# Linear attention scan of a two-layer hybrid block: six query scalings in one VectorE instruction, the decay column copied by ScalarE

## The chip, the cores and the metric

One NeuronCore of one Trainium2 chip runs the whole program. The metric is the device time of one execution in microseconds (us). Each execution is one launch; a version is judged by the median of its timed runs. One execution is also recorded by the hardware profiler, and all rows below come from that one record.

## The reference

The block has two layers. Each normalises 1024 latent and 256 context tokens, projects them, runs four mixers (differential attention, mLSTM, gated linear attention, windowed attention), gates and projects back. The change touches the gated linear attention (GLA) alone:

```
def _gla_step(smat, xs):          # one chunk of one direction, all heads
    q, k, v, la = xs
    bc = jnp.cumsum(la, axis=2)
    inter = jnp.einsum('bhtd,bhdv->bhtv', q * jnp.exp(bc), smat)
    rel = jnp.where(tril[:, :, None], bc[:, :, :, None, :] - bc[:, :, None, :, :], -jnp.inf)
    a = jnp.einsum('bhtd,bhtsd,bhsd->bhts', q, jnp.exp(rel), k)
    o = inter + jnp.einsum('bhts,bhsv->bhtv', a, v)
    b_end = bc[:, :, -1]
    smat = jnp.exp(b_end)[..., None] * smat + jnp.einsum('bhsd,bhsv->bhdv', k * jnp.exp(b_end[:, :, None] - bc), v)
    return smat, o
```

It runs forward and backward over context and latents, with 4 heads of 32 key and 64 value channels. The decay is different for each channel and token, so that q and k have to be scaled by exponentials before they are multiplied.

## The kernel before, in words

Tokens are cut into 10 tiles of 128, and each tile is visited once in each direction: 20 units a layer, in the order of the list UNITS, which alternates the two directions. The arrays q and k lie transposed (128 channels by tokens, qT and kT). For unit u the scan does five things.

- TensorE, `exponents(u)` (lines 1219 to 1224): six matmuls sum the log decays into eight 128x128 maps in PSUM banks 4 and 5.
- ScalarE (L1206): one Exp over all eight maps (128x1024) into `decays`, which has two places (u % 2) in the tile yT.
- GpSimd: `kx` = decays 1 to 5 times kT (L1194, 128x640), and place 0 from decay 0 and the token-major k (L1196, 128x128). VectorE, `scale_q(u)`: the last column of decay 7 is copied to `start` (L1303, 128x1, four places); `qx` = decays 2 to 6 times qT (L1304, 128x640, two places); `from_start` = decay 7 times qT (L1306, 128x128, three places).
- TensorE, `levels(u)` (L1237, L1242, L1248): the score maps of four heads at several distances, from kx and qx into PSUM banks 0 to 3. `fresh(u)` (L1260): the new state's sum from kx place 0. `out(u)`: from_start times the state (L1271), plus the picked scores times v (L1274).
- VectorE: three masked copies of the scores from PSUM into `acc`, here called the picks (L1335, 128x512 each). Then `finish(u)`: the state is scaled by `start` and the new sum added (L1312), and the output is copied to or added to yT (L1318 or L1316). After a wait for its own writes it marks `finished`.

The order on each engine is written out by hand. TensorE: exponents(0), exponents(1), then for each u levels(u), fresh(u), exponents(u+2), out(u-1), and last out(19). VectorE, for each u: finish(u-2), scale_q(u+1), picks(u). GpSimd and ScalarE take the units in turn. Semaphores tie them: levels(u) waits for its kx and qx and for the picks of u-1 (whose PSUM banks it overwrites); picks(u) wait for levels(u); finish(u) waits for out(u) and fresh(u); Exp(u) waits for the exponents and for both scalings of u-2; scale_q(u) waits for Exp(u), for levels(u-2) and, from u = 3, for out(u-3).

No DMA that the scan waits for is issued in it, and a barrier of all engines closes it. One scan runs in each layer; the two are at 409 to 522 us and 1774 to 1887 us of the record.

Of the kernel before, what the change touches and what calls it, by code (L numbers as in the profile page):

```python
# [999 lines left out]
def stage_gla(nc, env):  # L1000
# [3 lines left out]
    with outer:  # L1004
# [19 lines left out]
        with ExitStack() as own, nc.Block() as block:  # L1024
# [101 lines left out]
            def _(dve):  # L1126
# [21 lines left out]
                for n, b in enumerate(BLOCKS):  # L1148
# [3 lines left out]
                dve.wait_ge(k_kept.sem, 3)  # L1152


        (sums_ready, expo_mm, decay_ready, k_scaled, q_scaled, map_mm, picked, o_mm, u_mm, finished, zeroed, cleared, dv2) = (
            signal(n) for n in ("c_sums_ready", "c_expo_mm", "c_decay", "c_k_scaled", "c_q_scaled", "c_map_mm",
                                "c_picked", "c_out_mm", "c_new_mm", "c_finished", "c_zeroed", "c_cleared", "c_dve2"))
        NU = len(UNITS)
        with ExitStack() as own, nc.Block() as block:
            def tile(name, shape, dt=F32):  # L1160
                return own.enter_context(env["sbuf"](name, shape, dt))

            sums = tile("c_sums", [P, 2, 8 * P], F32R)
            decays = yT[:, 6:8, :].rearrange("p a t -> p (a t)")[:, 0:2 * 8 * P].rearrange("p (u n t) -> p u n t", u=2, n=8)
            kx = tile("c_kx", [P, 2, 6, P])
            qx = tile("c_qx", [P, 2, 5, P])
            from_start = tile("c_from_start", [P, 3, P])

            spare = env["ring"][:, S_AV % RING, KT * SLAB_W[S_AV]:]
            acc = spare[:, 0:2 * HEADS * P].rearrange("p (w h t) -> p w h t", w=2, h=HEADS)  # L1170
            state = spare[:, 2 * HEADS * P:2 * HEADS * P + 2 * GW].rearrange("p (w c) -> p w c", w=2)
            start = tile("c_start", [P, 4])

            def out_bank(u):
                return ps[:, 6 + u % 2, 0:GW]
# [4 lines left out]
            def span(u):  # L1180
                return slice(UNITS[u][2] * P, (UNITS[u][2] + 1) * P)

            @block.gpsimd
            def _(pool):
                pool.tensor_copy(sums[:, 1, :], sums_in[:, 8 * P:]).then_inc(sums_ready.sem, 1)
                pool.wait_ge(sums_ready.sem, 2)
                pool.memset(acc[:, :, :, :], 0.0).then_inc(zeroed.sem, 1)
                pool.memset(state[:, :, :], 0.0).then_inc(zeroed.sem, 1)
                for u in range(NU):
                    pool.wait_ge(decay_ready.sem, u + 1)  # L1190
                    if u >= 2:
                        pool.wait_ge(map_mm.sem, u - 1)
                        pool.wait_ge(u_mm.sem, u - 1)
                    pool.tensor_tensor(kx[:, u % 2, 1:6, :], decays[:, u % 2, 1:6, :],  # L1194
                                       kT[:, span(u)].unsqueeze(1).broadcast_to([P, 5, P]), ALU.mult).then_inc(k_scaled.sem, 1)
                    pool.tensor_tensor(kx[:, u % 2, 0, :], decays[:, u % 2, 0, :], k_tok[:, UNITS[u][2], :], ALU.mult)\  # L1196
                        .then_inc(k_scaled.sem, 1)

            @block.scalar
            def _(act):  # L1200
                for u in range(NU):
                    act.wait_ge(expo_mm.sem, u + 1)
                    if u >= 2:
                        act.wait_ge(k_scaled.sem, 2 * (u - 1))
                        act.wait_ge(q_scaled.sem, 2 * (u - 1))
                    act.activation(decays[:, u % 2, :, :], ps[:, 4:6, :].rearrange("p b (n t) -> p (b n) t", n=4), ACT.Exp)\  # L1206
                       .then_inc(decay_ready.sem, 1)

            @block.tensor
            def _(pe):  # L1210
# [15 lines left out]

                def levels(u):
                    way, i, j = UNITS[u]
                    q, k = qx[:, u % 2, :, :], kx[:, u % 2, :, :]
                    pe.wait_ge(k_scaled.sem, 2 * u + 1)  # L1230
                    pe.wait_ge(q_scaled.sem, 2 * u + 1)
                    if u >= 1:
                        pe.wait_ge(picked.sem, 3 * u)
                    for n, (a, b) in enumerate(((4, 2), (5, 3), (1, 4))):
                        for h in range(HEADS):
                            r = slice(32 * h, 32 * h + 32)
                            pe.matmul(ps[:, h, n * P:(n + 1) * P], k[r, a, :], q[r, b, :], start=True, stop=True,  # L1237
                                      tile_position=(32 * h, 0))
                    s0, t0 = (0, 64) if way == 0 else (64, 0)
                    for h in range(HEADS):  # L1240
                        r = slice(32 * h, 32 * h + 32)
                        pe.matmul(ps[s0:s0 + 64, h, t0:t0 + 64], k[r, 2, s0:s0 + 64], q[r, 0, t0:t0 + 64],  # L1242
                                  start=True, stop=True, tile_position=(32 * h, s0))
                    for blk in (0, 64):
                        s0, t0 = (blk, blk + 32) if way == 0 else (blk + 32, blk)
                        for h in range(HEADS):
                            r = slice(32 * h, 32 * h + 32)
                            last = pe.matmul(ps[s0:s0 + 32, h, t0:t0 + 32], k[r, 3, s0:s0 + 32], q[r, 1, t0:t0 + 32],  # L1248
                                             start=True, stop=True, tile_position=(32 * h, s0))
                    last.then_inc(map_mm.sem, 1)  # L1250
# [13 lines left out]
                def out(u):  # L1264
# [2 lines left out]
                        pe.wait_ge(zeroed.sem, 2)  # L1267
                    if u >= 2:
                        pe.wait_ge(finished.sem, u - 1)
                    pe.wait_ge(q_scaled.sem, 2 * (u + 1))  # L1270
                    pe.matmul(out_bank(u), from_start[:, u % 3, :], state[:, way, :], start=True, stop=False, skip_group_check=True)  # L1271
                    pe.wait_ge(picked.sem, 3 * (u + 1))
                    for h in range(HEADS):
                        last = pe.matmul(out_bank(u)[:, h * DH:(h + 1) * DH], acc[:, way, h, :], vC[:, j, h * DH:(h + 1) * DH],  # L1274
# [15 lines left out]
            def _(dve):  # L1290
# [3 lines left out]
                def scale_q(u):  # L1294
                    way, i, j = UNITS[u]
                    dve.wait_ge(decay_ready.sem, u + 1)
                    if u >= 2:
                        dve.wait_ge(map_mm.sem, u - 1)
                    if u >= 3:
                        dve.wait_ge(o_mm.sem, u - 2)  # L1300
                    end = P - 1 if way == 0 else 0
                    d = decays[:, u % 2, :, :]
                    dve.tensor_copy(start[:, u % 4:u % 4 + 1], d[:, 7, end:end + 1])  # L1303
                    dve.tensor_tensor(qx[:, u % 2, :, :], d[:, 2:7, :], qT[:, span(u)].unsqueeze(1).broadcast_to([P, 5, P]), ALU.mult)\  # L1304
                       .then_inc(q_scaled.sem, 1)
                    dve.tensor_tensor(from_start[:, u % 3, :], d[:, 7, :], qT[:, span(u)], ALU.mult).then_inc(q_scaled.sem, 1)  # L1306

                def finish(u):
                    way, i, j = UNITS[u]
                    dve.wait_ge(u_mm.sem, u + 1)  # L1310
                    dve.wait_ge(o_mm.sem, u + 1)
                    dv2.mark(dve.scalar_tensor_tensor(out=state[:, way, :], in0=state[:, way, :], scalar=start[:, u % 4:u % 4 + 1],  # L1312
# [1137 lines left out]
```

## Time and profile before

| | |
|---|---|
| three timed runs | 2673.01, 2687.75, 2691.18 us; median 2687.75 |
| the profiled execution's own time | 2683.7 us |
| its span | 2681.9 us (1.8 us lie around it) |
| mean granted TensorE clock | 0.88 of full speed |
| TensorE matmul busy | 2151.8 us, 80% of the span |
| VectorE busy | 1867.3 us, 70% |
| ScalarE busy | 1129.8 us, 42% |
| GpSimd busy | 411.4 us, 15% |

An engine's busy share is an average over eight stages a layer with different limits, so it does not say what bounds the scan. The granted clock is 1.00 where TensorE runs at 2.4 GHz and 0.50 where it runs at 1.2 GHz. In the rows, PE is TensorE's matmuls, PEld its weight loads, DVE is VectorE, ACT is ScalarE, POOL is GpSimd; L1304 is line 1304.

### The profile page before, as it was taken

The page shows a single profiled execution, that of the slowest core. Times are in us where ns is not written, and L with a number is a line of the kernel's source. Part 1 is how long each engine was busy: PE and PEld are TensorE (multiplying, and loading weights), DVE is VectorE, ACT ScalarE, POOL GpSimd, SP SyncE. Part 2 cuts the span into 40 slices and gives each one's busy share as a digit, 9 for nine tenths or more (in the row PEclk, how much of TensorE's full clock was granted, in tenths as well). Part 3 has the DMA queues.
Part 4 walks back from the last instruction along what each step waited for, and adds up shares of the span by engine and source line. Part 5 has one row for each costly group of instructions (what it writes and reads, how often), then busy time and mean ns, then how long its engine had stood idle before and what let it go on. Part 6 is the DMA issues. An engine that isn't in the chain of part 4 may idle for free. (4 is left out here: it accounts for less than half of the span.)

```text
span 2681.9 us, 38569 instructions
## 1 busy us (share of the span) xinstructions
PE 2151.8 (80%) x14712; PEld 1804.3 (67%) x14712; DVE 1867.3 (70%) x3533; ACT 1129.8 (42%) x2196; POOL 411.4 (15%) x410
## 2 busy tenths in 40 slices
PE   4968798786888785899978778879767977858988
PEld 2857676666677664787857567767655866647877
DVE  2585667778878567755745766669698786667757
ACT  4433351333667534633224443432435666346321
POOL 0002204322000011022110004025031000110222
PEclk7978896898898797999988889969788989979999
DMA  8100010000000100001433000100000001000021
GB/s 322 74 16 1 17 48 2 2 1 1 1 1 1 48 32 1 29 36 39 153 138 120 16 16 2 48 16 2 1 0 1 1 1 48 16 17 27 37 104 54
DMA packets 18182, 99.80 MB, mean 37 GB/s; under 512 B 2128, under 2 KB 2256, under 8 KB 12752
## 3 DMA queue, kind: packets, MB, share of 16 engines
q1 hardware_dynamic: 12816, 87.89, 8.6%
q10 hardware_dynamic: 5184, 9.44, 0.9%
q8 instruction: 119, 1.95, 0.3%
q14 instruction: 63, 0.52, 0.1%
HBM read 87.88 MB, written 9.44 MB: 36 GB/s over the span
## 5 line engine op out<-in xcount | busy, mean ns | idle before, releaser
L1807 DVE TENSOR_REDUCE a_st<-ps 128x1 f32<-128x1280 f32 (+1 forms) x144 | 196.9, 1370 | 23.2 <-PE ps L1719 22.7
L1778 ACT ACTIVATE ring<-ps,a_st 128x1280 f32<-128x1280 f32 (+1 forms) x144 | 177.3, 1232 | 74.6 <-DVE a_st L1807 74.4
L454 PE MATMUL ps<-a_proj_wh,a_proj_xh 128*128 128x512 f32 (+1 forms) x320 | 119.2, 373 | 62.5 <-DVE a_proj_xl L435 61.6
L2090 PE MATMUL ps<-g_x_hi,g_w_hi 128*128 128x512 f32 (+1 forms) x400 | 148.4, 371 | 10.0 <-DVE g_x_lo L2151 9.5
L2091 PE MATMUL ps<-g_x_lo,g_w_hi 128*128 128x512 f32 (+1 forms) x400 | 147.7, 369 | 0.0
L2092 PE MATMUL ps<-g_x_hi,g_w_lo 128*128 128x512 f32 (+1 forms) x400 | 147.6, 369 | 0.0
L1719 PE MATMUL ps<-a_k,a_q 128*128 128x512 f32 (+1 forms) x400 | 123.8, 419 | 26.1 <-ACT ring L1778 21.6
L2151 DVE TENSOR_TENSOR g_x_lo<-hT,g_x_hi 128x512 fp32r<-128x512 f32 (+1 forms) x120 | 84.5, 709 | 85.3 <-ACT g_x_hi L2114 83.8
L2114 ACT ACTIVATE g_x_hi<-hT 128x512 fp32r<-128x512 f32 (+1 forms) x120 | 70.3, 589 | 158.3 <-PE ps L2092 151.2
L1734 PE MATMUL ps<-cst,ring 128*128 128x128 f32 x656 | 107.8, 299 | 27.0 <-ACT a_aT L1787 15.1
L418 ACT ACTIVATE b_proj_xh<-hT 128x640 fp32r<-128x640 f32 (+1 forms) x64 | 63.8, 1003 | 147.4 <-PE ps L454 145.0
L2225 PE MATMUL ps<-o_w_hi,o_y_hi 128*128 128x512 f32 x288 | 114.1, 396 | 13.5 <-DVE o_y_lo L2256 7.2
L2164 POOL TENSOR_TENSOR yT<-yT,g_gate 128x512 f32<-128x512 f32 (+1 forms) x50 | 61.3, 1232 | 382.5 <-DVE g_gate L2129 236.7
L454 PEld LDWEIGHTS ps<-a_proj_wh,a_proj_xh 128*128 128x128 f32 x320 | 68.7, 215 | 75.3 <-issue 48.9
L454 PE MATMUL ps<-a_proj_wl,a_proj_xh 128*128 128x512 f32 (+1 forms) x320 | 116.2, 363 | 0.0
L454 PE MATMUL ps<-a_proj_wh,a_proj_xl 128*128 128x512 f32 (+1 forms) x320 | 115.8, 362 | 0.0
L2226 PE MATMUL ps<-o_w_lo,o_y_hi 128*128 128x512 f32 x288 | 113.5, 394 | 0.0
L2227 PE MATMUL ps<-o_w_hi,o_y_lo 128*128 128x512 f32 x288 | 113.3, 393 | 0.0
L1734 PEld LDWEIGHTS ps<-cst,ring 128*128 128x128 f32 x656 | 81.4, 153 | 46.5 <-ACT a_aT L1787 22.9
L454 PE MATMUL ps<-b_proj_xh,b_proj_wh 128*128 128x512 f32 (+1 forms) x192 | 76.9, 401 | 44.4 <-DVE b_proj_xl L435 38.0
L418 ACT ACTIVATE a_proj_xh<-hT 128x640 fp32r<-128x640 f32 x64 | 46.6, 741 | 147.9 <-PE ps L454 145.6
L2282 ACT ACTIVATE o_y_hi<-yT 128x640 fp32r<-128x640 f32 (+1 forms) x64 | 43.5, 686 | 152.5 <-PE ps L2227 144.6
(363 smaller groups left out, 6397.9 us busy)
## 6 DMA issues: line engine op xcount, KB each, us to landing
ring<-in_w SPq DMA_DIRECT2D x22, 2048.0 KB, 7.5
yT<-in_w SPq DMA_DIRECT2D x4, 2048.0 KB, 9.8
latents<-hT ACTq DMA_DIRECT2D x32, 256.0 KB, 2.0
ring<-in_w SPq DMA_DIRECT2D x6, 1024.0 KB, 5.0
hT<-in_tok SPq DMA_DIRECT2D x10, 512.0 KB, 15.5
hT<-in_tok SPq DMA_DIRECT2D x20, 256.0 KB, 5.9
hT<-latents SPq DMA_DIRECT2D x16, 256.0 KB, 6.5
cst<-in_cst SPq DMA_DIRECT2D x1, 2688.0 KB, 14.6
```

The lines of the kernel that those rows point to most:

```text
L418: act.activation(self.x_hi[:, i % self.BUFS, 0:m], self.env["hT"][:, k, t0:t0 + m], ACT.Copy).then_inc(self.hi.sem, 1)
L454: last = pe.matmul(out, left, right, start=k == 0 and j == 0, stop=k == KT - 1 and j == 2)
L1719: last = pe.matmul(ps[:, 3 * c + b, 0:w], q4[:, 2 * h + c, t * P:(t + 1) * P], k4[:, 2 * h + c, k0:k0 + w], start=True, stop=True)
L1734: last = pe.transpose(ps[:, 6 + n % 2, (k - a) * P:(k - a + 1) * P], p(u, 0, T)[:, k * P:(k + 1) * P], C(env, "ident"))
L1778: act.activation(p(u, c, n), ps[:, 3 * c:3 * c + 3, :].rearrange("p b n -> p (b n)")[:, 0:n], ACT.Exp, bias=st[:, 0:1], accum_out=st[:, 1: ...
L1807: dve.tensor_reduce(stat[:, u % SLOTS, c, 0:1], ps[:, 3 * c:3 * c + 3, :].rearrange("p b n -> p (b n)")[:, 0:n], AX.X, ALU.max, negate=Tru ...
L2090: pe.matmul(out, w_hi[:, k, cols], x_hi[:, at, 0:b[1]], start=k == 0, stop=False)
L2091: pe.matmul(out, w_hi[:, k, cols], x_lo[:, at, 0:b[1]], start=False, stop=False)
L2092: last = pe.matmul(out, w_lo[:, k, cols], x_hi[:, at, 0:b[1]], start=False, stop=k == KT - 1)
L2225: pe.matmul(ps[:, n % 8, :], y_hi[:, at, tile], w_hi[:, at, :], start=k == 0, stop=False)
L2226: pe.matmul(ps[:, n % 8, :], y_hi[:, at, tile], w_lo[:, at, :], start=False, stop=False)
L2227: last = pe.matmul(ps[:, n % 8, :], y_lo[:, at, tile], w_hi[:, at, :], start=False, stop=k == KT - 1)
```

## The change

`decays` leaves yT: place 0 becomes a tile of its own and place 1 goes to the spare part of the ring, where `state` was; `state` becomes a tile of its own. `qx` moves into yT, has three places instead of two and six maps instead of five, and takes the place of `from_start`. VectorE makes all six products in one instruction (128x768). The copy of the decay column moves from VectorE to ScalarE, as an activation (Copy) behind the Exp, with a semaphore `start_kept` for which `finish` waits. The counts of `q_scaled` go by one a unit instead of two; scale_q(u) waits for levels(u-3) instead of levels(u-2).

```diff
-            decays = yT[:, 6:8, :].rearrange("p a t -> p (a t)")[:, 0:2 * 8 * P].rearrange("p (u n t) -> p u n t", u=2, n=8)
             kx = tile("c_kx", [P, 2, 6, P])
-            qx = tile("c_qx", [P, 2, 5, P])
-            from_start = tile("c_from_start", [P, 3, P])
+            qx = yT[:, 6:8, :].rearrange("p a t -> p (a t)")[:, 0:3 * 6 * P].rearrange("p (u n t) -> p u n t", u=3, n=6)
...
-            state = spare[:, 2 * HEADS * P:2 * HEADS * P + 2 * GW].rearrange("p (w c) -> p w c", w=2)
+            decays = [tile("c_decays", [P, 8, P]), spare[:, 2 * HEADS * P:2 * HEADS * P + 8 * P].rearrange("p (n t) -> p n t", n=8)]
+            state = tile("c_state", [P, 2, GW])
...
             def _(act):
...
                     if u >= 2:
                         act.wait_ge(k_scaled.sem, 2 * (u - 1))
-                        act.wait_ge(q_scaled.sem, 2 * (u - 1))
-                    act.activation(decays[:, u % 2, :, :], ps[:, 4:6, :].rearrange("p b (n t) -> p (b n) t", n=4), ACT.Exp)\
+                        act.wait_ge(q_scaled.sem, u - 1)
+                    act.activation(decays[u % 2][:, :, :], ps[:, 4:6, :].rearrange("p b (n t) -> p (b n) t", n=4), ACT.Exp)\
                        .then_inc(decay_ready.sem, 1)
+                    end = P - 1 if UNITS[u][0] == 0 else 0
+                    act.wait_ge(decay_ready.sem, u + 1)
+                    if u >= 4:
+                        act.wait_ge(finished.sem, u - 3)
+                    act.activation(start[:, u % 4:u % 4 + 1], decays[u % 2][:, 7, end:end + 1], ACT.Copy).then_inc(start_kept.sem, 1)
...
                 def levels(u):
-                    q, k = qx[:, u % 2, :, :], kx[:, u % 2, :, :]
+                    q, k = qx[:, u % 3, :, :], kx[:, u % 2, :, :]
                     pe.wait_ge(k_scaled.sem, 2 * u + 1)
-                    pe.wait_ge(q_scaled.sem, 2 * u + 1)
+                    pe.wait_ge(q_scaled.sem, u + 1)
...
-                    pe.wait_ge(q_scaled.sem, 2 * (u + 1))
-                    pe.matmul(out_bank(u), from_start[:, u % 3, :], state[:, way, :], start=True, stop=False, skip_group_check=True)
+                    pe.wait_ge(q_scaled.sem, u + 1)
+                    pe.matmul(out_bank(u), qx[:, u % 3, 5, :], state[:, way, :], start=True, stop=False, skip_group_check=True)
...
                 def scale_q(u):
                     dve.wait_ge(decay_ready.sem, u + 1)
-                    if u >= 2:
-                        dve.wait_ge(map_mm.sem, u - 1)
                     if u >= 3:
+                        dve.wait_ge(map_mm.sem, u - 2)
                         dve.wait_ge(o_mm.sem, u - 2)
-                    end = P - 1 if way == 0 else 0
-                    d = decays[:, u % 2, :, :]
-                    dve.tensor_copy(start[:, u % 4:u % 4 + 1], d[:, 7, end:end + 1])
-                    dve.tensor_tensor(qx[:, u % 2, :, :], d[:, 2:7, :], qT[:, span(u)].unsqueeze(1).broadcast_to([P, 5, P]), ALU.mult)\
+                    dve.tensor_tensor(qx[:, u % 3, :, :], decays[u % 2][:, 2:8, :], qT[:, span(u)].unsqueeze(1).broadcast_to([P, 6, P]), ALU.mult)\
                        .then_inc(q_scaled.sem, 1)
-                    dve.tensor_tensor(from_start[:, u % 3, :], d[:, 7, :], qT[:, span(u)], ALU.mult).then_inc(q_scaled.sem, 1)
 
                 def finish(u):
+                    dve.wait_ge(start_kept.sem, u + 1)
                     dve.wait_ge(u_mm.sem, u + 1)
                     dve.wait_ge(o_mm.sem, u + 1)
```

## Rows read from the trace of the kernel before

**Rows 1.** Busy time by stretch (us, PE, PEld, DVE, ACT, POOL, clock, DMA), first scan.
```profile
430.00:440.00 10.00, 10.00 (x130) 8.36 (x129) 6.22 (x14) 1.02 (x1) 2.64 (x4) 0.50 0.01 2
...
450.00:460.00 10.00, 9.29 (x186) 7.84 (x179) 9.13 (x18) 2.05 (x2) 5.80 (x6) 1.00 0.02 4
```

**Rows 2.** Waits in 449 to 510 us: who waited, total us, times, longest.
```profile
ACT yT L1206 <- PE ps L1224: 45.9, 13, 3.6
...
PE ps L1237 <- DVE ring L1335: 5.0, 14, 0.4
```

**Rows 3.** Timeline, one full-clock iteration: start us, us, engine, line, idle before.
```profile
449.03 0.46 DVE L1312 SCALAR_TENSOR_TENSOR ring<-ring,c_start,ps 128x256 f32<-128x256 f32 x1
...
502.55 1.00 PE L1274 MATMUL ps<-yT,ring 128*128 128x64 f32 x8
...
503.42 1.55 POOL L1194 TENSOR_TENSOR c_kx<-yT,c_kT 128x640 f32<-128x640 f32 x1 [2.01 <-ACT yT L1206]
503.66 0.48 DVE L1312 SCALAR_TENSOR_TENSOR ring<-ring,c_start,ps 128x256 f32<-128x256 f32 x1
...
503.87 0.95 PE L1237 MATMUL ps<-c_qx,c_kx 32*128 32x128 f32 x24 [0.32 <-DVE ring L1335]
504.06 0.42 DVE L1316 TENSOR_TENSOR yT<-ps,yT 128x256 f32<-128x256 f32 x1
504.72 0.15 DVE L1303 COPY c_start<-yT 128x1 f32<-128x1 f32 x1 [0.24 <-DVE yT L1316]
...
504.79 0.86 DVE L1304 TENSOR_TENSOR c_qx<-yT,c_qT 128x640 f32<-128x640 f32 x1
...
505.57 0.55 DVE L1306 TENSOR_TENSOR c_from_start<-yT,c_qT 128x128 f32<-128x128 f32 x1
...
506.04 2.25 DVE L1335 COPY_PREDICATED ring<-cst,ps 128x512 f32<-128x512 uint32 x3
...
507.07 1.00 PE L1274 MATMUL ps<-yT,ring 128*128 128x64 f32 x8
...
508.19 0.47 DVE L1312 SCALAR_TENSOR_TENSOR ring<-ring,c_start,ps 128x256 f32<-128x256 f32 x1
...
508.44 0.95 PE L1237 MATMUL ps<-c_qx,c_kx 32*128 32x128 f32 x24 [0.37 <-DVE ring L1335]
```

**Rows 4.** Durations ns, min/median/max, of single lines in 449 to 510 us.
```profile
L1304 DVE TENSOR_TENSOR c_qx<-yT,c_qT x14: 814/864/904, 450.1 to 509.3; 128x640 f32<-128x640 f32 x14
...
L1306 DVE TENSOR_TENSOR c_from_start<-yT,c_qT x13: 279/546/549, 450.9 to 505.6; 128x128 f32<-128x128 f32 x13
...
L1196 POOL TENSOR_TENSOR c_kx<-yT,c_k_tok x14: 460/1050/1069, 450.2 to 509.4; 128x128 f32<-128x128 f32 x14
```

**Rows 5.** Timeline, at the granted clock of 0.50 and where it rises.
```profile
437.48 0.48 DVE L1312 SCALAR_TENSOR_TENSOR ring<-ring,c_start,ps 128x256 f32<-128x256 f32 x1 [2.80 <-PE ps L1274]
...
442.90 1.81 PE L1274 MATMUL ps<-yT,ring 128*128 128x64 f32 x8
...
444.81 0.48 DVE L1312 SCALAR_TENSOR_TENSOR ring<-ring,c_start,ps 128x256 f32<-128x256 f32 x1 [2.79 <-PE ps L1274]
```

**Rows 6.** Timeline, the first units of the scan.
```profile
414.21 1.57 POOL L1194 TENSOR_TENSOR c_kx<-yT,c_kT 128x640 f32<-128x640 f32 x1 [2.01 <-ACT yT L1206]
414.23 2.22 DVE L1304 TENSOR_TENSOR c_qx<-yT,c_qT 128x640 f32<-128x640 f32 x1
...
419.75 0.55 DVE L1306 TENSOR_TENSOR c_from_start<-yT,c_qT 128x128 f32<-128x128 f32 x1
...
420.21 2.24 DVE L1335 COPY_PREDICATED ring<-cst,ps 128x512 f32<-128x512 uint32 x3
...
422.60 1.66 PE L1237 MATMUL ps<-c_qx,c_kx 32*128 32x128 f32 x24 [1.04 <-DVE ring L1335]
```

**Rows 7.** Timeline, levels of the last unit.
```profile
512.93 1.66 PE L1237 MATMUL ps<-c_qx,c_kx 32*128 32x128 f32 x24 [1.32 <-DVE ring L1335]
```

**Rows 8.** Line 995, a ScalarE Copy behind an Exp, whole record (ns min/median/max).
```profile
L995 ACT ACTIVATE yT<-ps,par x108: 360/424/523, 312.5 to 2277.2; 128x128 f32<-128x128 f32 x108
```

More of the change, by code:

```diff
@@ L1152, in _ @@
                 dve.wait_ge(k_kept.sem, 3)
-        (sums_ready, expo_mm, decay_ready, k_scaled, q_scaled, map_mm, picked, o_mm, u_mm, finished, zeroed, cleared, dv2) = (
+        (sums_ready, expo_mm, decay_ready, k_scaled, q_scaled, map_mm, picked, o_mm, u_mm, finished, zeroed, cleared, dv2, start_kept) = (
             signal(n) for n in ("c_sums_ready", "c_expo_mm", "c_decay", "c_k_scaled", "c_q_scaled", "c_map_mm",
-                                "c_picked", "c_out_mm", "c_new_mm", "c_finished", "c_zeroed", "c_cleared", "c_dve2"))
+                                "c_picked", "c_out_mm", "c_new_mm", "c_finished", "c_zeroed", "c_cleared", "c_dve2", "c_start_kept"))
         NU = len(UNITS)
@@ L1193, in _ @@
                         pool.wait_ge(u_mm.sem, u - 1)
-                    pool.tensor_tensor(kx[:, u % 2, 1:6, :], decays[:, u % 2, 1:6, :],
+                    pool.tensor_tensor(kx[:, u % 2, 1:6, :], decays[u % 2][:, 1:6, :],
                                        kT[:, span(u)].unsqueeze(1).broadcast_to([P, 5, P]), ALU.mult).then_inc(k_scaled.sem, 1)
-                    pool.tensor_tensor(kx[:, u % 2, 0, :], decays[:, u % 2, 0, :], k_tok[:, UNITS[u][2], :], ALU.mult)\
+                    pool.tensor_tensor(kx[:, u % 2, 0, :], decays[u % 2][:, 0, :], k_tok[:, UNITS[u][2], :], ALU.mult)\
                         .then_inc(k_scaled.sem, 1)
```

## The prediction

> **What bounds the kernel now.** The scan fills 112.9 us in each of the two layers, 226 of 2682 us, so I looked only there, first at the busy time by stretch. It shows two regimes [rows 1]. At a granted clock of 0.50 TensorE is busy without a gap. At 1.00 it is busy 93% and VectorE 91%: either could be the bound, and shares cannot say which. Next the waits [rows 2]: at full clock the levels' matmuls wait for the picks in each of 14 iterations, 0.36 us a time, while ScalarE has 3.5 us of idle time an iteration. Last the timeline of one iteration [rows 3], in which every start and end can be chained.
>
> The start of the finish's first instruction, L1312, moves from 449.03 to 508.19 in 13 iterations: 4.55 us each. Call E the end of the `out` matmuls, 502.55 + 1.00 = 503.55. VectorE's next steps, counted from E [rows 3]: L1312 at +0.11, the output at +0.51, the column copy at +1.17, qx at +1.24, from_start at +2.02, the picks at +2.49 to +4.74. The next but one `levels` starts at 508.44, +4.89, and TensorE needs 4.20 us from the start of levels to its own `out` end (503.87 to 507.07 + 1.00 = 508.07). This gives a **loop over two iterations**: out, finish, scalings, picks, levels, out. Its length is 4.89 + 4.20 = 9.09, or 4.545 an iteration. VectorE's own list, L1312 to L1312, takes 508.19 - 503.66 = 4.53. TensorE's own takes 4.20. So two loops bind at once, within 0.02 us. Shortening VectorE's list relieves the first as well, but the first holds the VectorE stretch only once in two iterations.
>
> **The change, part by part.**
>
> The column copy leaves VectorE: qx starts 0.07 after it [rows 3]. It saves at most 0.07 an iteration, and nothing where the port below decides.
>
> The two products become one. From the undisturbed lengths, 814 ns for 640 elements and 279 for 128 [rows 4], an element costs 535/512 = 1.045 ns. So 768 elements take 0.948, or 0.134 more than 640. from_start's slot goes: 506.04 - 505.57 = 0.47. It is so long because VectorE and GpSimd exclude each other here. L1306 takes 279 or 546 ns and L1196 460 or 1050 [rows 4], and in the first unit qx takes 2.22 where L1194 started 0.02 before it [rows 6]: it is through 0.67 after L1194's end. The slot thus was 0.20 of work and 0.27 of waiting for L1196.
>
> In the sum the same exclusion takes a part back. L1194 runs until 503.42 + 1.55 = 504.97, E + 1.42, because it follows Exp, which follows TensorE's exponents: it stands still against E. qx is ready at E + 1.17 now and has to wait until E + 1.42. It ended at 505.65, 0.68 after that, and will end 0.68 + 0.13 = 0.81 after, at E + 2.23; the picks start 0.08 before it is through (505.57 against 505.65), at E + 2.15 instead of 2.49. Gain 0.34 for each turn of the two-iteration loop: (9.09 - 0.34) / 2 = 4.375, **0.17 us an iteration**. VectorE's own list falls to about 4.53 - 0.34 = 4.19 and no longer binds alone. Without the exclusion the picks would start at E + 1.17 + 0.87 = E + 2.04, the gain would be 0.45 a turn. The Trainium skill, page "SBUF — State Buffer", says of the port pair that the two engines share that a VectorE instruction with two SBUF inputs and a GpSimd one exclude each other for their whole length. By that rule the first sum holds, without it the second; the trace agrees with the rule, by the 2.22 us above.
>
> Sum for one layer:
> - Start. The first picks wait for from_start of unit 1, 419.75, and begin at 420.21; merged they begin at about 419.75 + 0.13 = 419.88, 0.33 sooner. levels(1), 422.60, waits for them and for nothing else (1.04 idle) [rows 6]. Its qx waits for the same L1194 as now. -0.33. levels(0) waits for the wider qx, +0.13, but the picks behind it still begin later than it ends, so this is covered.
> - Clock of 0.50. An iteration is 7.33 long and VectorE waits 2.8 in it for `out` [rows 5]. The saving is hidden: 0.
> - Full clock, from the finish at 444.81 to that at 508.19, 14 iterations, 7 turns of the loop. Six save 0.34. The first is undisturbed by GpSimd (from_start took its shortest 0.28), so it saves 0.07 + 0.20 - 0.13 = 0.14. Together -2.18; I take -2.2.
> - Tail. levels(19) at 512.93 waits for picks(18) [rows 7], one more VectorE stretch behind the out end at 508.07. -0.34.
>
> That is -2.9 a layer, **-5.8 us** for both.
>
> At nothing I put: the ScalarE copy, 40 times. The nearest row is a Copy of 128x128 in 0.42 us behind an Exp, with no table load on its line [rows 8]; it lies in 3.5 us of idle time [rows 2], and a cost below nothing is excluded, since ScalarE does more. Its wait for finish(u-4) was met some 3 us before. If the cover were gone, each copy would delay the next Exp by at most 0.42 us. Behind Exp, GpSimd waits for decay_ready, which Exp itself still signals. The new wait of finish(u) for start_kept: the copy is done a full iteration before; the wait is issued while the last pick still runs. Between nothing and one semaphore step (0.11, out end to L1312) I take nothing; what queues behind it is all of VectorE's list, and at 0.11 a turn it would cost 7 x 0.11 a layer, 1.5 us in all. Three places of qx and the later levels wait (u-3 for u-2): VectorE never idled for it, 0. The widened qx holds L1196 up by 0.13, but fresh(u) needs it more than 3 us later. Moved tiles: no row prices an address; I take 0, and -1 to +1 us as ends. No DMA changes.
>
> **The rivals.**
>
> *A, the full width of VectorE's list.* If the end of `out` modelled in the trace is later than the real one, the two-iteration loop has slack and only the one-engine lists bind. VectorE's is then 4.53 - 0.47 - 0.07 + 0.13 = 4.12, TensorE's 4.20 + a step of 0.03, so TensorE paces at 4.23: 0.32 x 14 + 0.67 = 5.1 a layer, -10 us. For it: a matmul's end is modelled in the record, not seen. Against: out end to L1312 is 0.11 here and 444.81 - (442.90 + 1.81) = 0.10 where VectorE really waited [rows 5].
>
> *B, no gain.* TensorE at 93% is near its bound; if levels start later for another reason (kx, semaphores), the 0.17 vanishes: 0 to -2 us. Against: in all 14 iterations the wait ends with the picks [rows 2].
>
> *C, slower by the port.* qx wins the port now because it is already waiting when L1194 ends. If it comes after that, L1196 gets in first and qx waits another 0.46: picks at E + 1.42 + 0.46 + 0.81 - 0.08 = E + 2.61, against 2.49 now. The loop grows by 0.12 a turn, with the start's gain left: 7 x 0.12 - 0.33 = +0.5 a layer, **+1 us**, at worst +2. The point is qx ready later than E + 1.42; it is ready at E + 1.17, 0.07 sooner than now. The long L1306 is the rule (median 546), the short one the exception. Small.
>
> *D, the clock.* It rises when TensorE has run without a gap for some iterations [rows 1, 5]. The start's gap before levels(1) shrinks by 0.33 and everything after shifts. One iteration more at 0.50 costs 7.33 - 4.38 = 3 us a layer, and one fewer saves it: 2 x 3 on either side, -12 or 0. If later stages shift their rises too, slower by a few us is possible. The Trainium skill, "TensorE: Matmul & The Clock Gate", Part 1, says that idle TensorE is throttled and activity releases it; by that fewer gaps can only help, and I give the side of later rises less. This trace cannot tell them apart.
>
> **How the numbers follow.** The change is made against the profiled execution, 2683.7 us, which lies 4 us below the median of the three runs. The forecast for the profiled time is 2677.9, for the median 2687.75 - 5.8 = **2682 us**. The forecast itself, -4 to -7: 0.56. A: 0.12. B: 0.13. C: 0.05. D faster 0.07, D slower 0.07. The three runs spread over 18 us, more than any case; a median can move by that much with no change at all. The range goes from A on the lowest run (2673 - 10 = 2663, taken as 2665) to C on the highest (2691 + 2 = 2693). A change of less than 1% (27 us) can hardly be told from none in this kernel. Even all of 0.47 + 0.07 - 0.13 = 0.41 us in 40 units would be 16 us, so faster by over 1% needs the clock: 0.03. Slower by over 1% needs several later rises: 0.03. The rest, 0.94, is within 1%.
>
> **What would show it.** Right: L1312 to L1312 4.35 to 4.40 us at full clock; one qx row of 128x768 of 0.95 undisturbed and about 1.05 where it waits for L1194; picks at E + 2.15; the levels' wait for the picks down from 0.36 to about 0.18; a new wait of L1312 for `out` of 0.1 to 0.2; the same number of slow iterations; no second table load in the scan; each scan 110.0 instead of 112.9 us. Wrong: iterations of 4.23 (A), of 4.5 with TensorE's wait on something else (B), 0.46 us long L1196 before qx and picks at E + 2.6 (C), another count of 7.33 us iterations (D).

## The result and the profile after

| | us |
|---|---|
| before, median of 8 runs (2673.01 to 2691.18) | 2684.6 |
| changed, median of 8 runs (2650.28 to 2665.72) | 2658.6 |
| ratio of the runs | 0.9906, 95% interval 0.9883 to 0.9929 |
| forecast | 2682 (2665 to 2693), within 1% |

The time is below the range: some 25 us gained where 5.8 were forecast. A second timing gave 0.9925 (0.9907 to 0.9942), 20 us. The profiled run took 2660.28 us, 23.4 less than the one before. Two lines of its page:

```profile
span 2658.5 us, 38559 instructions
...
PE 2129.9 (80%) x14712; PEld 1785.4 (67%) x14712; DVE 1850.4 (70%) x3453; ACT 1137.3 (43%) x2236; POOL 418.2 (16%) x410
```

Where the time went is seen by cutting the span at the scans. Scan length here is from the first VectorE instruction to the start of the last finish (L1312). Each is a difference of two timeline rows; for the second scans these are 1886.47 - 1774.51 and 1864.27 - 1764.69.

| record | first scan | second scan | the rest of the span |
|---|---|---|---|
| before | 111.9 | 112.0 | 2458.0 |
| changed | 103.0 | 99.6 | 2455.9 |

So 21.3 of the 23.4 us lie in the scans of these two records. Inside them, first the steady part, which answers [rows 3]. This is the timeline of the changed kernel at full clock (start us, us, engine, line, idle before):

```profile
436.13 1.00 PE L1278 MATMUL ps<-yT,ring 128*128 128x64 f32 x8
...
437.00 1.55 POOL L1193 TENSOR_TENSOR c_kx<-ring,c_kT 128x640 f32<-128x640 f32 x1 [1.89 <-ACT ring L1205]
...
437.13 0.95 PE L1241 MATMUL ps<-yT,c_kx 32*128 32x128 f32 x24
437.27 0.48 DVE L1312 SCALAR_TENSOR_TENSOR c_state<-c_state,c_start,ps 128x256 f32<-128x256 f32 x1 [0.29 <-ACT c_start L1211]
...
438.33 1.05 DVE L1304 TENSOR_TENSOR yT<-ring,c_qT 128x768 f32<-128x768 f32 x1 [0.24 <-DVE yT L1316]
...
439.30 2.26 DVE L1335 COPY_PREDICATED ring<-cst,ps 128x512 f32<-128x512 uint32 x3
...
440.32 1.00 PE L1278 MATMUL ps<-yT,ring 128*128 128x64 f32 x8
...
441.45 0.48 DVE L1312 SCALAR_TENSOR_TENSOR c_state<-c_state,c_start,ps 128x256 f32<-128x256 f32 x1
```

With E = 436.13 + 1.00 = 437.13, L1312 stands at E + 0.14, qx at + 1.20, the picks at + 2.17 (forecast + 2.15). qx takes 1.05 because L1193 holds the port until 438.55. VectorE now waits 0.29 for `out`. The row names the column copy as releaser, since that ended last by the profile (437.16); but finish(u) needs the copy of its own unit, which was long done. Experiment 5 has no such copy, and there the same wait is put down to `out`. From 430 to 500 us of this record the levels wait for the picks 8 times in 16 iterations, 3.3 us in all or 0.21 an iteration (forecast 0.18), and L1312 waits in the others, 0.34 a time (forecast 0.1 to 0.2).

From levels(2) at 20.17 to levels(18) at 90.23 us of the first scan there are 16 iterations: 4.38 us each. Before, levels(4) to levels(18), 35.47 to 99.27, were 14 of 4.56. Forecast were 4.375 and 4.545.

Now the clock. Busy time by stretch (us, PE, PEld, DVE, ACT, POOL, clock, DMA), second scan of before, in the 17.0 us that follow 18.4 us after its begin:

```profile
1792.90:1809.90 17.00, 17.00 (x155) 14.65 (x153) 8.17 (x17) 3.07 (x3) 5.10 (x5) 0.50 0.00 1
1809.90:1873.70 63.80, 58.86 (x1010) 50.80 (x1009) 59.19 (x113) 14.34 (x14) 34.55 (x29) 1.00 0.01 2
```

The same stretch of the changed kernel, and the 4.8 us ahead of it:

```profile
1778.20:1783.00 4.80, 4.80 (x64) 3.94 (x61) 3.10 (x4) 0.34 (x2) 2.73 (x2) 0.50 0.02 3
1783.00:1800.00 17.00, 15.99 (x286) 13.88 (x285) 14.21 (x22) 4.72 (x8) 9.20 (x8) 1.00 0.01 2
```

In 17 us TensorE does 155 matmuls at 1.2 GHz and 286 at 2.4. Before, the rise comes 35.4 us after the begin of both scans; changed, 19.8 and 18.4 us after it. That is the larger part of the difference between these two records.

The head of the scan shows what the rise may hang on. Timeline of the changed kernel, its first units; they answer [rows 6]:

```profile
413.19 0.96 DVE L1304 TENSOR_TENSOR yT<-c_decays,c_qT 128x768 f32<-128x768 f32 x1 [2.84 <-ACT c_decays L1205]
...
413.24 2.32 POOL L1193 TENSOR_TENSOR c_kx<-c_decays,c_kT 128x640 f32<-128x640 f32 x1 [2.01 <-ACT c_decays L1205]
...
416.67 2.34 DVE L1304 TENSOR_TENSOR yT<-ring,c_qT 128x768 f32<-128x768 f32 x1 [2.52 <-ACT ring L1205]
418.94 2.24 DVE L1335 COPY_PREDICATED ring<-cst,ps 128x512 f32<-128x512 uint32 x3
...
421.33 1.66 PE L1241 MATMUL ps<-yT,c_kx 32*128 32x128 f32 x24 [1.91 <-DVE ring L1335]
```

In unit 0 VectorE now has the port first, by 0.05 us, and GpSimd's product takes 2.32 instead of 1.57; in unit 1 it is the other way round. Either way the slower of the two ends at about the same time of the scan as before (7.36 us against 7.28), so levels(0) starts at 7.41 us of the scan against 7.43. levels(1) starts at 421.33 - 408.20 = 13.13 instead of 422.60 - 409.17 = 13.43: 0.30 sooner (forecast 0.33).

### The profile page after: what moved, and what is told of

Its sections match the earlier page's. It is cut to its first block and busy times, and to the rows that moved or that the text cites. A ratio compares the mean times of both kernels' runs of the same rounds, so it can differ in the third digit from the quotient of the medians.

```text
span 2658.5 us, 38559 instructions
## 1 busy us (share of the span) xinstructions
PE 2129.9 (80%) x14712; PEld 1785.4 (67%) x14712; DVE 1850.4 (70%) x3453; ACT 1137.3 (43%) x2236; POOL 418.2 (16%) x410
## 5 line engine op out<-in xcount | busy, mean ns | idle before, releaser
L2225 PE MATMUL ps<-o_w_hi,o_y_hi 128*128 128x512 f32 x288 | 114.2, 396 | 13.4 <-DVE o_y_lo L2256 7.2
```

The lines of the kernel that those rows point to most:

```text
L2225: pe.matmul(ps[:, n % 8, :], y_hi[:, at, tile], w_hi[:, at, :], start=k == 0, stop=False)
```

## Experiments

Each was timed against the kernel before on the same chip; kernels 1 to 4, 5 to 8, 9 to 11 and 12 ran on four different chips, so between these groups it is the ratios that compare. "Rise" is when the granted clock goes from 0.50 to 1.00 for good, in us of the scan. The kernels are numbered in the order of running; all compute the full result, and filler results are read by nobody.

| kernel | median us (runs) | ratio to before, 95% | scans in the record | rise | rest of the span |
|---|---|---|---|---|---|
| 1 before again | 2679.5 (12) | 1.0003 (0.9987-1.0018) | 105.6, 112.0 | 19.7, 35.4 | 2459.8 |
| 2 changed again | 2659.6 (5) | 0.9925 (0.9907-0.9942) | 103.0, 99.5 | 19.7, 18.4 | 2455.2 |
| 3 before, filled | 2656.7 (4) | 0.9911 (0.9895-0.9927) | 99.7, 103.3 | 4.7, 18.3 | 2451.4 |
| 4 changed, filled | 2649.9 (6) | 0.9888 (0.9868-0.9907) | 98.6, 98.5 | 4.7, 4.7 | 2457.4 |
| 5 merge only | 2662.6 (6) | 0.9927 (0.9912-0.9942) | 99.6, 99.5 | 18.4, 18.4 | 2455.8 |
| 6 copy only | 2679.7 (12) | 1.0000 (0.9989-1.0010) | 105.5, 112.0 | 19.7, 35.4 | 2460.5 |
| 7 before, head | 2669.1 (6) | 0.9958 (0.9944-0.9971) | 102.6, 105.2 | 19.7, 18.4 | 2459.5 |
| 8 changed, late | 2670.4 (7) | 0.9963 (0.9949-0.9977) | 103.2, 99.9 | 19.7, 18.6 | 2461.8 |
| 9 changed, port | 2657.9 (6) | 0.9918 (0.9896-0.9940) | 99.1, 98.9 | 19.7, 14.9 | 2457.5 |
| 10 filled, tail | 2655.8 (6) | 0.9913 (0.9896-0.9929) | 95.5, 97.7 | 4.7, 14.8 | 2461.3 |
| 11 filled, tail, port | 2652.1 (6) | 0.9901 (0.9885-0.9918) | 95.2, 97.3 | 6.0, 15.0 | 2457.9 |
| 12 changed, late, again | 2666.3 (11) | 0.9952 (0.9937-0.9967) | 103.2, 99.9 | 19.7, 18.6 | 2460.2 |

### Both kernels again (1 and 2)

> The kernel before, unchanged, for a second profile and for the granted clock of each run. Theory 1 (the clock decides, and the change moves its rise): the 3 to 4 iterations of 7.3 us at the head of each scan come back in this second record, levels(1) to levels(4) 22 us apart. Theory 2 (the moment of the rise is chance, and the first record of before was an unlucky one): another number of 7.3 us iterations, and the spread of the runs is that chance. Both: time equal to before, 2684 us, within 5 us; full-clock iterations of 4.55 us.

> The changed kernel, unchanged, for a second profile. Theory 1: again only one or two iterations of over 6 us at the head of each scan, scans of 101 to 104 us from the first VectorE instruction to the last finish, 2658 us, -25 against before. Theory 2: the number of slow iterations changes freely between the two records. Both: mean full-clock iteration 4.38 us.

Half of each reading holds. The changed kernel repeats itself to 0.1 us in both scans. Before repeats its second scan, rise at 35.4, but in the first the clock rose at 19.7 this time. Its second scan in this record, from 18.3 us on, again without a gap on TensorE:

```profile
1788.40:1805.40 17.00, 17.00 (x155) 14.69 (x153) 8.26 (x17) 3.07 (x3) 4.98 (x5) 0.50 0.00 1
```

The first scan of the same record, with the rise at 426.5:

```profile
420.30:426.50 6.20, 6.20 (x68) 5.25 (x68) 3.77 (x5) 1.02 (x1) 1.55 (x3) 0.50 0.00 0
426.50:442.30 15.80, 14.64 (x274) 12.63 (x275) 13.80 (x28) 3.07 (x3) 8.97 (x8) 1.00 0.01 2
```

So the size of the gain differs from one execution of before to the next: 21.3 us in the scans against its first record, 15.0 against its second.

The scans also differ in the granted clock ahead of them, counted from the records' clock. In the first scans of kernels 1 and 2 it had last fallen 7.6 us before the scan's begin, and from there it takes the same course in both: at 1.00 from 9.5 to 12.9 us, up for good at 19.7. These two are the pair with an equal clock, up to the tail. The start of their last finish and the full-clock stretch of kernel 2:

```profile
512.42 0.48 DVE L1312 SCALAR_TENSOR_TENSOR ring<-ring,c_start,ps 128x256 f32<-128x256 f32 x1 [1.74 <-PE ps L1274]
...
510.54 0.48 DVE L1312 SCALAR_TENSOR_TENSOR c_state<-c_state,c_start,ps 128x256 f32<-128x256 f32 x1 [1.74 <-PE ps L1278]
...
427.30:502.30 75.00, 70.50 (x1222) 60.99 (x1221) 66.61 (x103) 19.63 (x32) 44.36 (x34) 1.00 0.01 2
```

From their begins at 406.81 and 407.52 that is 105.6 and 103.0 us: 2.6 us for the change (3.1 up to levels(18), of which the tail gives 0.5 back; forecast 2.9 a layer), and no earlier rise. Where the clock had last fallen 5.5 to 5.6 us before the scan's begin, both scans of before's first record and the second ones of kernels 1 and 6 rise at 35.4, but the second ones of both records of the changed kernel, and both of kernel 5, rise at 18.4. So in these records the change moves the rise only in scans of this second kind. Before's first record had two of them and its second record had one, and that makes the two gains differ.

### Clock made equal by filler (3 and 4)

```diff
                     last.then_inc(k_turned.sem, 1)
+                for _ in range(16):
+                    pe.matmul(ps[:, 5, 0:P], C(env, "ident"), C(env, "ones"), start=True, stop=True)
...
+                def filler(n, at=ps[:, 0, 3 * P:4 * P]):
+                    for _ in range(n):
+                        pe.matmul(at, C(env, "ident"), C(env, "ones"), start=True, stop=True)
+
+                filler(4)
                 exponents(0)
+                filler(2)
                 exponents(1)
                 for u in range(NU):
+                    if u == 1:
+                        filler(2, ps[:, 7, 0:P])
                     levels(u)
```

> The kernel before with idle TensorE filled at the head of the scan: 16 matmuls of 128x128 on constants behind the last transposes of the stage before, 4 ahead of exponents(0), 2 ahead of exponents(1), 2 ahead of levels(1); they write PSUM that nobody reads. They cost at most about 1 us a scan where they reach past a wait. Theory 1 (most of the 26 us is the clock at the head of the scans, and filled gaps raise it): iterations of 7.3 us go from 3 to 0 or 1 a scan, each worth 2.8 us, so -12 to -18 us against before, with full-clock iterations still 4.55. Rival (the gain is in the shorter VectorE list itself): no gain from filling, 0 to +4 us, the slow iterations stay.

> The same filling in the changed kernel. Theory 1: with the clock equal in both, what is left between this and the filled kernel before is the list's own share that was forecast, 5 to 8 us; against the changed kernel it gains only the one or two slow iterations that are left, -3 to -8 us, so about 2652 us. Rival: it keeps the whole 25 us distance from the filled kernel before.

Filler alone gives the kernel before what the change gave: -0.89%, with its VectorE list untouched. Of the 23 us, 14.6 lie in the scans of the two records and 8.4 outside them, more than theory 1 expected. Between the two filled kernels lie 2656.7 - 2649.9 = 6.8 us by the medians and 203.0 - 197.1 = 5.9 us in the scans of the records. That this is close to the 5.8 forecast for the list is luck, since the clock was not equal: kernel 3 fell back to 0.50 for 3.4 us in its second scan (below), and kernel 4 lost some 3 us in the tail of its first, where it took 12.8 us and kernel 3 took 9.7. Equal was the clock from 4.7 us on to levels(18) in the first scans. levels(18) of kernel 3, whose scan began at 409.04, and of kernel 4, which began at 409.01:

```profile
499.10 0.95 PE L1239 MATMUL ps<-c_qx,c_kx 32*128 32x128 f32 x24 [0.28 <-DVE ring L1345]
...
494.78 0.95 PE L1243 MATMUL ps<-yT,c_kx 32*128 32x128 f32 x24
```

That is 90.06 and 85.77 us of the scan: 4.3 us for the list with 17 iterations at full clock, 3.0 of them in the iterations (4.55 to 4.37 us each) and 1.3 ahead of levels(1). The filled kernel before at work in its first scan (the same columns; its iterations from levels(6) to levels(18) are still 4.56 us):

```profile
413.80:444.40 30.60, 25.69 (x434) 21.84 (x433) 28.23 (x48) 7.43 (x8) 17.14 (x15) 1.00 0.01 2
```

The filled changed kernel in that stretch:

```profile
413.80:444.40 30.60, 27.75 (x493) 23.69 (x493) 24.76 (x37) 9.03 (x16) 21.21 (x16) 1.00 0.01 2
```

In the second scan of kernel 3 the clock was up at 4.7 us, fell at 14.9 and rose for good at 18.3: filler does not hold it for certain.

### The two halves of the change (5 and 6)

Kernel 5 is the changed kernel without ScalarE's copy and the wait for it:

```diff
-                    act.activation(start[:, u % 4:u % 4 + 1], decays[u % 2][:, 7, end:end + 1], ACT.Copy).then_inc(start_kept.sem, 1)
...
+                    dve.tensor_copy(start[:, u % 4:u % 4 + 1], decays[u % 2][:, 7, end:end + 1])
...
-                    dve.wait_ge(start_kept.sem, u + 1)
```

> One half of the change: the six products in one instruction and the new places, but the column copy stays on VectorE ahead of them. Theory 1 (the wider product lets the picks of unit 0 and so levels(1) begin 0.3 us sooner, and with the fuller head of the scan the clock rises some 15 us earlier): nearly the whole gain, -18 to -25 us; levels(1) at 13.1 to 13.2 us of the scan, full clock from about 20 us on in both scans, full-clock iterations 4.38. Rival (the copy's move is what counts, since it decides who gets the port first in unit 0): -5 us or less.

Kernel 6 is the kernel before with ScalarE's copy instead of VectorE's, in the same words the other way round.

> The other half: only the column copy moves to ScalarE, the products stay 5 + 1. Theory 1: full-clock iterations stay at 4.50 to 4.55 us (the copy's slot is 0.07 at most), levels(1) about 0.07 sooner or not at all, slow iterations as before in most scans; 0 to -5 us. Rival: VectorE wins the port in unit 0 as in the changed kernel, the rise comes earlier, -10 us or more.

The merged product is the change: -17 us by the medians of this chip (just short of the -18 to -25 expected), and its record has the fast scans. The copy's move is worth nothing by itself (interval -0.11% to +0.10%). Moving it did let VectorE have the port first in unit 0, with no gain: the port's rival is out. The waits of kernel 5 at full clock (430 to 500 us; who waited for whom, total us, times, longest):

```profile
PE ps L1236 <- DVE ring L1331: 3.0, 8, 0.7
...
DVE c_state L1308 <- PE ps L1273: 1.7, 7, 0.3
```

Here the finish waits for `out` (L1273) in every second iteration. That is the two-iteration loop: one side waits, then the other.

### One instruction moved at the head (7), and the head made late (8 and 12)

```diff
-                    dve.tensor_tensor(from_start[:, u % 3, :], d[:, 7, :], qT[:, span(u)], ALU.mult).then_inc(q_scaled.sem, 1)
+                    if u != 1:
+                        scale_start(u)
...
                     for n in range(3):
...
+                    if u == 0:
+                        scale_start(1)
```

> The kernel before with one instruction of each scan moved: the single product (from_start) of unit 1 is issued behind the picks of unit 0 instead of ahead of them. All other units as before. It lets levels(1) begin about 0.45 us sooner and does nothing else. Theory 1 (a gap at the head moves the rise): full clock from 20 us on instead of 35 in most scans, iterations of 4.55 after it, -8 to -16 us in all for half a microsecond. Rival (the rise is chance, or comes from the denser iterations): 0 to -2 us, the rise at 35 us.

levels(1) starts at 13.00 instead of 13.43 us, the rise comes at 19.7 and 18.4, and the whole program is 10 us faster (0.9958) for one moved instruction a scan. Against kernel 6's record, which repeats before's times, the scans are 9.7 us shorter: 6.8 in the second, where the rise moved, and 2.9 in the first, where the rise stands at 19.7 in both and the tail stayed at full clock. Its second scan, in the 17 us in which the kernel before stood at 0.50:

```profile
1785.00:1802.00 17.00, 15.65 (x284) 13.52 (x284) 14.59 (x29) 3.67 (x4) 9.12 (x8) 1.00 0.01 2
```

The counter-test puts idle work into the changed kernel:

```diff
+            late = tile("c_late", [P, 320])
...
+                    if u == 0:
+                        dve.memset(late[:, :], 0.0)
                     dve.wait_ge(map_mm.sem, u + 1)
```

> The changed kernel with 0.33 us of VectorE work that nobody reads (a memset of 128x320) ahead of the picks of unit 0, so that levels(1) begins as late as in the kernel before (13.4 us of the scan). Theory 1: the early rise is lost in most scans, +8 to +14 us against the changed kernel (2666 to 2673 us), iterations of 4.38 after it. Rival: +1 us, the rise stays at 18 to 20 us.

> The changed kernel with 0.33 us of idle work ahead of the picks of unit 0, a second record. Open is why its runs were 10 us slower than the changed kernel's while its first record showed early rises in both scans. Reading 1 (the first record was one of the lucky ones and the late levels(1) often delays the rise): this record has the clock rising at 35 us in one scan at least. Reading 2 (the delay is lost outside the scans, where the first record had 6 us more between them): rises at 18 to 20 us again, and 4 to 7 us more than the changed kernel's 1253.4 us between the scans. Both: median 2667 to 2673 us.

The times went as theory 1 had it (+7 to +11 us against the changed kernel), but the records do not show its mechanism. levels(1) is late, at 13.41, yet the clock rises at 19.7 and 18.6, twice alike:

```profile
1789.60:1806.40 16.80, 15.72 (x285) 13.60 (x284) 13.68 (x21) 4.73 (x8) 8.58 (x8) 1.00 0.01 2
```

Both records lose their time outside the scans: between them lie 1259.9 us both times, against 1253.4 in both records of the changed kernel. By the granted clock of the records, 287.1 us of this stretch are at 0.50 in both, against 270.4, so the loss goes with the clock there too. Reading 2 of the last expectation holds. Had I only had the medians, I would have taken this as a confirmation.

But the late head is not refuted as a cause of the late rise, because in the second scans the clock came later as well. The stretch from its last fall to the scan's begin, and the first matmuls of levels(1), in the second scan of before and then of kernel 8:

```profile
1768.95:1774.51 5.56, 0.00 (x0) 0.00 (x0) 4.86 (x9) 0.04 (x1) 0.03 (x1) 0.50 0.00 0
1787.95 0.60 PE L1237 MATMUL ps<-c_qx,c_kx 32*128 32x128 f32 x4 [1.05 <-DVE ring L1335]
...
1765.70:1771.01 5.31, 0.00 (x0) 0.00 (x0) 4.61 (x9) 0.04 (x1) 0.02 (x1) 0.50 0.00 0
1784.42 0.60 PE L1242 MATMUL ps<-yT,c_kx 32*128 32x128 f32 x4 [1.04 <-DVE ring L1338]
```

Counted from that fall of the clock, levels(1) begins after 18.98 to 19.01 us in all four scans with the rise at 35.4, after 18.73 and 18.75 in the second scans of kernels 8 and 12, and after 18.51 to 18.66 in the five scans with the rise at 18.4. Seen so, the idle work brought levels(1) only 0.1 us nearer to before, and not the 0.3 that the scan's own time shows. No run tests that distance by itself.

### The port and the tail (9, 10, 11)

```diff
                         pool.wait_ge(u_mm.sem, u - 1)
+                    pool.wait_ge(q_scaled.sem, u + 1)
                     pool.tensor_tensor(kx[:, u % 2, 1:6, :], decays[u % 2][:, 1:6, :],
```

> The changed kernel with one wait more: GpSimd's product kx of a unit waits until VectorE's qx of the same unit is through, so that VectorE never waits for the port. Theory 1 (two-iteration loop with the port in it): picks start at out end + 2.04 us instead of + 2.15, full-clock iterations of (8.75 - 0.11) / 2 = 4.32 us instead of 4.38; at the head qx of unit 1 takes 0.95 us instead of 2.34 and levels(1) begins up to 0.8 us sooner; -2 to -4 us against the changed kernel. Rival (GpSimd's later kx delays levels): iterations of 4.45 or more, and a wait of levels for kx.

All 40 qx now take their undisturbed time. From kernel 9's lines (ns min/median/max):

```profile
L1305 DVE TENSOR_TENSOR yT<-c_decays,c_qT x20: 957/959/960, 413.6 to 1852.5; 128x768 f32<-128x768 f32 x20
L1305 DVE TENSOR_TENSOR yT<-ring,c_qT x20: 957/959/961, 417.1 to 1857.1; 128x768 f32<-128x768 f32 x20
```

Timeline of kernel 9 at full clock, the end of `out` and the picks after it:

```profile
471.04 1.00 PE L1279 MATMUL ps<-yT,ring 128*128 128x64 f32 x8
...
474.12 2.28 DVE L1336 COPY_PREDICATED ring<-cst,ps 128x512 f32<-128x512 uint32 x3
```

The picks start at 472.04 + 2.08, which is 0.09 sooner than in the changed kernel (expected 0.11). Iterations fall from 4.38 to 4.35 us (levels(2) to levels(18), 69.6 / 16), where 4.32 was expected, and the rival's 4.45 did not come. levels(1) starts 0.53 sooner. So the port was in the loop, with a share of a few hundredths. The scans are 4.6 us shorter in sum, but 3.2 of that are a tail at full clock in the first one (9.6 for 12.8 us), which the port does not explain; by the medians the difference to the changed kernel is not measurable.

```diff
+                    if u == NU - 1:
+                        pe.wait_ge(decay_ready.sem, NU)
+                        filler(5, ps[:, 4, 0:P])
```

> The filled changed kernel with 5 more filler matmuls in the gap of 1.2 to 1.4 us ahead of levels(19). If that gap is what lets the clock fall before the last unit, both tails keep 2.4 GHz and take 9.6 us instead of 12.8 from levels(18) to the last finish: -3 to -6 us against the filled changed kernel of 2650 us. Rival: the fall comes after the scan's end in any case or the filler delays levels(19): 0 to +1 us.

> All three together: filler at the head, filler in the gap before the last unit, GpSimd's wait. Gains add if they are separate: iterations of 4.32 us, full clock from 5 us of the scan on, tails of 9.6 us: 2642 to 2648 us, -1.3% against the kernel before. Rival: GpSimd's wait costs at the head, since kx of units 0 and 1 comes later while the clock is up and TensorE is sooner there: no better than the filled kernel without it.

With the gap ahead of levels(19) filled, both tails (levels(18) to the last finish) take 9.7 us instead of the 12.8 of kernel 4, whose clock fell at 90.0 us of the scan, inside that gap, with levels(19) at 90.4. levels of the last unit, which took 1.66 us in [rows 7], in kernel 10:

```profile
499.18 0.95 PE L1243 MATMUL ps<-yT,c_kx 32*128 32x128 f32 x24 [0.29 <-DVE ring L1348]
```

In the first scan, where kernels 4 and 10 run alike up to levels(18), the gap is the only difference, so it was the reason for the fall there. But in the second scan of both kernels the clock fell once more at the head (rise for good at 14.8 and 15.0), and the rest of the span differs by 4 us between kernels 4 and 10, so no total gain shows: the medians are 2655.8 and 2652.1 us where some 2645 were expected, and the ratios are no lower than kernel 4's. Kernels 4 and 11, at -1.1% and -1.0%, are the fastest versions that ran; their intervals overlap with each other, and with the change's own.

## Why the prediction was wrong

**What bounds the scan: right.** The two-iteration loop gave 4.375 us, measured 4.38, where VectorE's own list alone would have given some 4.2 and TensorE's 4.20 to 4.23 (rival A, which is out). The picks start at E + 2.17 for E + 2.15.

**The merged product: right.** Undisturbed it takes 0.957 us (forecast 0.948); waiting for the port 1.05. The copy at nothing: right, kernel 6; it takes 0.20 us.

**Start and full clock: right in size; the tail: wrong.** Start 0.30 and 0.31 for 0.33. The 14 iterations from levels(4) to levels(18) took 63.8 us before and 61.3 after, -2.5 a layer; the forecast was -2.2. The tail's -0.34 did not come: in the first scans levels(18) to the last finish took 12.6 us before and 12.8 after. The changed iterations alternate between some 4.1 and 4.6 us, and levels(18) to levels(19) is one of the long ones, 4.6 us against 4.5 before: the last iteration is the half of the loop that the change did not shorten. With the clock equal (first scans of kernels 1 and 2) a scan is 2.6 us shorter for 2.9.

**The term "Clock of 0.50: the saving is hidden: 0" is the step that failed.** Hidden it was, but the stretch itself did not stay as long. In the first scan, levels(1) to levels(4) took 22.0 us before and 15.8 after; in the second 22.0 and 15.5. Of these 12.7 us, 0.7 are the faster list: two iterations a scan more run at full clock, each 0.18 shorter. The other 12.0 are the clock. About half of them are not the change's: in the first scan before's clock had last fallen 5.6 us ahead, the changed kernel's 7.5, and kernel 1, whose clock had fallen as the changed kernel's, took 16.0 us there. The second scan's 6.1 repeat in kernels 1 and 2. The second scan's tail stayed at full clock as well: from levels(18) to the last finish 9.7 instead of 12.8 us, 3.1 more. That makes 15.1 us of clock and 6.3 us of list (0.6 start, 5.0 and 0.7 iterations); measured in all 21.3.

**Rival D had the mechanism and the wrong price and chance.** It put one iteration of 3 us a scan on either side, with 0.07 for faster. The rise moved by more than two iterations a scan. What misled me was taking the rise as a fixed count of iterations that a shift could move by one. That it rises when TensorE has run without a gap for some iterations does not hold: it came 22 us after levels(1) in four scans and 6.2 us after it in two others of the same instructions. Two scans that looked the same, rise at 35.4 in both, made it look settled; the second record of before has one of them at 19.7. The sentence that fewer gaps can only help, which I drew from what the Trainium skill, page "TensorE: Matmul & The Clock Gate", Part 1, says of idle TensorE and activity, pointed the right way and was the one thing that should have raised the chance. Activity alone did not release the throttle here, though: the 22 us without a gap at 0.50 in four scans speak against the rule in its plain form. The prediction said that it gave later rises less, yet both sides of D got 0.07. That fewer gaps help is what filler shows on the chip: 23 us in all, 14.6 of them in the scans.

**The other rivals.** B and C did not come: no iteration of 4.5, and the picks were never at E + 2.6.

**What stays open.** The rise at 35.4 is seen in four scans: both of before's first record, and the second ones of kernels 1 and 6. In none of the 11 other records is it seen. It came only where the clock had last fallen 5.5 to 5.6 us ahead of the scan, and there in every scan of before and copy only, and in none with a merged product. What sets that fall was not tested. That the head decides is shown by kernel 7, which differs in one instruction and has the rise at 18.4 with the same fall ahead. What at the head decides is not: the start of levels(1), counted from the fall, orders these scans without an exception, but no run changed it alone. Nor is it explained why the same code between the scans takes 1253.4 us in one record and 1259.9 in another. It is not a property of the kernel alone: before took 1253.4 in one record and 1257.6 in the next. The slower of each two has more time at the granted clock of 0.50 (287.1 for 270.4 us, 278.0 for 273.8).

## What to carry to other kernels

Where two engines hand work back and forth, write down the loops that span several iterations as well as each engine's own list: a cut in one engine's list counts once for each turn of the longer loop, and here that gave the time of an iteration to 0.01 us. If a record shows stretches at the lower TensorE clock, price the change with the stretch at both lengths, and take a second record of the unchanged kernel before believing that its length is fixed, and compare stretches whose clock was alike, ahead of them too. Filler matmuls in both versions help to separate the two causes, but check in the records that the clock really was equal: a matching sum can be luck, as here. Cheap work in the gaps at the head of a stage may be worth as much as the edit itself.

## What the runs showed of the hardware

- TensorE ran 22 us without a gap at the granted clock of 0.50 before the clock rose (levels(1) at 13.4 to the rise at 35.4 us, in four scans of before and copy only). In two other scans of the same instructions (the first of kernels 1 and 6) it rose 6.2 us after levels(1), after a short spell at 1.00 from 9.5 to 12.9 us of the scan. Being busy was not enough for the rise.
- In both scans of kernel 4 the clock fell in a gap of some 1.5 us ahead of levels(19), and it stayed up in kernels 10 and 11 when the gap was filled. Without filler it went either way: the tail took 12.3 to 12.8 us in all scans of kernels 1 and 6, and 9.6 to 9.7 in both scans of kernel 5 and one of kernel 7.
- Which engine gets the port is decided by hundredths of a microsecond: 413.19 against 413.24 gave VectorE 0.96 and GpSimd 2.32; 416.64 against 416.67 gave GpSimd 1.56 and VectorE 2.34. The one that waits shows it as its own longer duration, not as idle time.
- The same code does not always take the same time: the part between the scans, in the kernels without filler, took 1252.0 to 1260.8 us, with 265 to 287 us of it at the granted clock of 0.50. Two records of one kernel agreed within 0.1 us (changed; changed, late) or differed by 4.2 (before).
